# A forget-gate scan, residual rows stored as they are scaled, more filler products, and slot tables of thirteen experts kept in device memory

## What is computed

```python
def fox_shared_kv(h, kv_w, forget_bias):
    k, v, fl = jnp.split(h @ kv_w, [FD, 2 * FD], axis=-1)        # fl: 512 x 16
    log_f = jax.nn.log_sigmoid(fl + forget_bias)
    return k, v, jnp.cumsum(log_f, axis=1)                       # over the tokens

def grouped_moe(x, router_w, router_bias, w_gate, w_up, w_down):
    ...                                                          # gates: 512 x 16, two not 0
    h = silu(einsum('td,edf->tef', x, w_gate)) * einsum('td,edf->tef', x, w_up)
    return einsum('tef,efd->td', h * gates[..., None], w_down)   # 16 experts, D 1024, F 512

h = layer_norm(ALPHA * h + mix, ...)
h = layer_norm(ALPHA * h + grouped_moe(h, ...), ...)
```

## Time and profile before

| | us |
|---|---|
| median of three executions | 1234.36 |
| lowest, highest | 1230.32, 1236.86 |
| profiled execution, its own time | 1230.52 |
| its span, first to last instruction | 1228.8 |
| busy TensorE, VectorE, ScalarE, GpSimd | 1193.8, 893.2, 703.7, 183.9 |
| mean granted TensorE clock | 0.992 |

### The profile page before, as it was taken

The page is one execution under the profiler, slowest core; times in us unless marked ns, Lnnn a source line. Parts: engine busy times, 40 slices in busy tenths (PEclk is TensorE's granted clock), DMA queues, the critical chain, the costliest instruction groups (busy, mean ns, idle before and its releaser), DMA issues.

```text
span 1228.8 us, 14990 instructions
## 1 busy us (share of the span) xinstructions
PE 1193.8 (97%) x5802; PEld 945.0 (77%) x5803; DVE 893.2 (73%) x1159; ACT 703.7 (57%) x866; POOL 183.9 (15%) x158
## 2 busy tenths in 40 slices
PE   7999999999999999999999999999999999999995
PEld 5787588877888888876887766768878888888873
DVE  5275555678999998989433555675679999998886
ACT  4432523357687786774333554573267778777672
POOL 1000100211132221210000000000212222122111
PEclk9999999999999999999899999999999999999998
DMA  8223021179999999987111420322289999999973
GB/s 286 71 85 122 1 103 70 52 257 411 358 368 378 368 370 377 358 340 281 69 70 52 154 86 18 103 84 88 78 314 381 373 362 376 379 367 371 370 276 137
DMA packets 66346, 281.52 MB, mean 229 GB/s; under 512 B 12854, under 2 KB 13110, under 8 KB 41698
## 3 DMA queue, kind: packets, MB, share of 16 engines
q1 hardware_dynamic: 49248, 247.55, 53.2%
q0 software_dynamic: 12288, 28.42, 8.1%
q10 hardware_dynamic: 4738, 4.57, 1.1%
HBM read 270.99 MB, written 25.20 MB: 241 GB/s over the span
## 4 chain that ended last, share of the span: by engine, by line
PE 83%; DMA 7%; DVE 6%; issue 2%; ACT 1%; POOL 0%; DVEq 0%; SPq 0%; ACTq 0%; POOLq 0%
PE ps L717 22%; PE ps L719 22%; PE ps L718 22%; DMA ring<-in_moe_w_up_dram 4%; PE ps L885 2%; PE ps L1168 2%; PE ps L1178 2%; DVE ring_r L1613 2%; PE ps L1191 2%; DMA ring<-in_moe_w_down_dram 1%; PE ps L894 1%; DMA ring<-in_kv_w_dram 1%; PE ps L822 1%; PE ps L1099 1%; PE ps L1087 1%
## 5 line engine op out<-in xcount | busy, mean ns | idle before, releaser
L1613 DVE TENSOR_TENSOR ring_r<-ring,ring_r 128x2048 fp32r<-128x2048 f32 x128 | 291.7, 2284 | 7.8 <-ACT ring_r L1346 7.8
L1346 ACT CAST ring_r<-ring 128x2048 fp32r<-128x2048 f32 x128 | 242.6, 1927 | 15.7 <-DMA ring<-in_moe_w_gate_dram 9.8
L718 PE MATMUL ps<-ring_r,xgT_r 128*128 128x512 f32 x528 | 205.9, 390 | 0.0
L1346 ACT CAST high_r<-ring 128x2048 fp32r<-128x2048 f32 x64 | 122.2, 1913 | 113.4 <-DMA ring<-in_moe_w_up_dram 113.4
L1613 DVE TENSOR_TENSOR ring_r<-ring,high_r 128x2048 fp32r<-128x2048 f32 x64 | 146.1, 2289 | 36.3 <-ACT high_r L1346 35.9
L613 POOL DMA_INDIRECT sum_rows<-arena,tokv x28 | 57.7, 2062 | 389.6 <-ACT arena L1399 389.6
L718 PEld LDWEIGHTS ps<-ring_r,xgT_r 128*128 128x128 f32 x528 | 99.3, 188 | 18.8
L717 PE MATMUL ps<-ring_r,xgT_r 128*128 128x512 f32 x272 | 109.1, 401 | 0.2 <-DVE ring_r L1613 0.2
L719 PE MATMUL ps<-ring_r,xgT_r 128*128 128x512 f32 x272 | 106.1, 390 | 0.0
L717 PE MATMUL ps<-high_r,xgT_r 128*128 128x512 f32 x256 | 102.9, 402 | 1.2 <-DVE xgT_r L1827 1.1
L717 PE MATMUL ps<-featT,ring_r 128*128 128x512 f32 x256 | 103.8, 405 | 0.0
(11 more groups left out here) (288 smaller groups left out, 2118.8 us busy)
## 6 DMA issues: line engine op xcount, KB each, us to landing
ring<-in_moe_w_gate_dram SPq DMA_DIRECT2D x64, 1024.0 KB, 12.2
ring<-in_moe_w_up_dram SPq DMA_DIRECT2D x64, 1024.0 KB, 13.0
ring<-in_moe_w_down_dram SPq DMA_DIRECT2D x64, 1024.0 KB, 12.4
ring<-in_gla_w_in_dram SPq DMA_DIRECT2D x6, 2048.0 KB, 9.8
ring<-in_kv_w_dram SPq DMA_DIRECT2D x4, 2048.0 KB, 12.8
ring<-in_fox_w_qg_dram SPq DMA_DIRECT2D x4, 2048.0 KB, 8.1
ring<-in_gla_w_out_dram SPq DMA_DIRECT2D x2, 2048.0 KB, 7.8
h_rows<-arena POOLq DMA_DIRECT2D x8, 512.0 KB, 2.9
```

The source lines that it names most:

```text
L718: pe.matmul(o, left[0], right[1], start=False, stop=False)
L1346: act.copy(high, w).then_inc(half_high, 1)
L1613: dve.tensor_tensor(low, w, high.bitcast(F32), ALU.subtract).then_inc(half_low, 1)
```

## The change

Five things, all at once:

1. Forget gates: `narrow` gives way to 24 products (8 blocks of three) with the 16 gate columns as weights and 512 tokens moving, so the result is 16 x 512 with the heads on partitions. Bias, Abs, Exp and Ln work on 16 x 512, and one scan of VectorE over the tokens gives the cumulative sum; the ten products and ScalarE's copy are gone.
2. Three of the four residual tiles are stored to `sum_rows` by ScalarE right after each is scaled.
3. The slot tables of experts 3 to 15 are made in device memory. VectorE works out for each token the two places expert + 16 x rank (`find_picks`, ten instructions), GpSimd writes (row number, gate) there by eight indirect stores and, when they have landed, loads the whole table, 128 x 16 x 2 (`store_picks`). The tables in device memory are filled with "no row" early in the program. One-hot comparisons, table products and `take_table` of the loop are gone; `TABLES` is 3.
4. `find_picks` stands before the first expert's rows are taken, and `take_rows(0)` before `low_half(L, 2)`.
5. More filler products at the entry: three, not two, after each of three row tables, two after each of three gate tables, then three, not five.

Some semaphores are merged (`gates_left` into `gates_summed`, `ids_done` into `tbl_done`), and two constants more are set by GpSimd at the start.

```diff
+    slot_tables = [nc.dram_tensor(f"slot_table{L}", [(P + 1) * E, 2], U32).ap() for L in range(DEPTH)]
...
+            def store_picks(L):
+                pool.wait_ge(picks_known, L + 1)
+                pool.wait_ge(tables_stored, 16 * (DEPTH + 2 * T * L))
+                for t in range(T):
+                    for j in range(2):
+                        pool.sem_inc(moves, 1)
+                        pool.indirect_dma_start(out=slot_tables[L],
+                                                out_offset=bass.IndirectOffsetOnAxis(ap=pick_at[:, t, j:j + 1], axis=0),
+                                                in_=pick_row[:, t, j, :], in_offset=None, bounds_check=last_slot,
+                                                oob_is_err=False).then_inc(tables_stored, 16)
+                pool.wait_ge(tables_stored, 16 * (DEPTH + 2 * T * (L + 1)))
+                pool.dma_start(slot_tab[:, :, :], slot_tables[L][E:, :].rearrange("(p e) c -> p e c", e=E)
+                               ).then_inc(slots_loaded, 16)
+                pool.wait_ge(slots_loaded, 16 * (L + 1))
...
+                store_picks(L)
                 for e in range(E + 1):
...
                     if e + 3 < E:
-                        pool.wait_ge(tbl_ev, 2 * (E * L + e + 4))
                         pool.wait_ge(xt_done, 2 * (E * L + e + 2))
-                        gather(xg[:, (e + 3) % 2, :], tokv[:, (e + 3) % TABLES, 0:1], gathered[(e + 3) % 2])
+                        gather(xg[:, (e + 3) % 2, :], rows_of(e + 3), gathered[(e + 3) % 2])
...
-                    entry_table(e, slice(0, 2), ps[:, IDS_BANKS[e], 0:2]).then_inc(ids_done, 1)
-                    idle_products(2, 4)
+                    entry_table(e, slice(0, 2), ps[:, IDS_BANKS[e], 0:2]).then_inc(tbl_done, 1)
+                    idle_products(3, 4)
                 pe.wait_ge(rt_ready, L + 1)
                 for e in range(3):
                     entry_table(e, slice(2, 4), ps[:, 6, 2 * e:2 * e + 2]).then_inc(tbl_done, 1)
-                idle_products(5, 4)
+                    idle_products(2, 4)
+                idle_products(3, 4)
...
-                    if e + 3 < E:
-                        pe.wait_ge(hot, E * L + e + 4)
-                        pe.wait_ge(tbl_ev, 2 * (E * L + e + 3))
-                        table(e + 3, onehot[:, (e + 3) % 2, :]).then_inc(tbl_done, 1)
...
-            for t in range(T):
-                mm = narrow(t, gkf)
+            for k in range(K):
+                mm = products(ps[0:H_B, 6, :], (gkf[:, k, 0, :], gkf[:, k, 1, :]), hT_block(k, slice(0, S)), k)
             mm.then_inc(fl_done, 1)
...
                 act.mul(dealt(H[:, t, :], K), blocks(Hp[:, t, :], K), ALPHA).then_inc(h_scaled, 1)
+                if t < T - 1:
+                    begin_sums(L, t)
+
+            def begin_sums(L, t):
+                act.wait_ge(h_scaled, T * L + t + 1)
+                act.dma_start(sum_rows[t * P:(t + 1) * P, :], H[:, t, :]).then_inc(sums_begun, 16)
...
+            def find_picks(L):
+                slot_of, far, by_pick = rt[0], rt[2], at(14656 + 64 * 4, 2 * T, E)
...
+                do(dve.scalar_tensor_tensor(out=slot_of, in0=ranks[:, :, 0:E], scalar=float(E),
+                                            in1=iota_e[:, :].unsqueeze(1).to_broadcast([P, T, E]),
+                                            op0=ALU.mult, op1=ALU.add))
...
+                dve.tensor_reduce(pick_gate[:, :, :, 1], four, AX.X, ALU.add).then_inc(picks_known, 1)
...
+                find_picks(L)
+                take_rows(0)
                 low_half(L, 2)
-                take_rows(0)
...
-                    if e + 3 < E:
-                        dve.wait_ge(tbl_done, E * L + e + 2)
-                        one_hots4(dve, onehot_of(e + 3), hot, ranks, slot1, e + 3)
...
-                    dve.tensor_tensor(f_log, f_log, f_tmp, ALU.subtract).then_inc(f_ready, 1)
+                    dve.tensor_tensor_scan(cumT[0:H_B, :], f_log, f_tmp, 0.0, ALU.add, ALU.subtract).then_inc(cum_ev, 1)
```

More of the change, by code:

```diff
@@ L674, in experts @@
                     inverse_deviation(2 * L + 1, t)
+            pool.wait_ge(kt_done, 1)
+            for L in range(DEPTH):
+                pool.dma_start(slot_tables[L][E:, :].rearrange("(p e) c -> p e c", e=E), no_slots[:, :, :]
+                               ).then_inc(tables_stored, 16)
             pool.wait_ge(sq_done, T * H_A)
@@ L759, in marker @@
                           ).then_inc(w_free, frees)
-            def narrow(t, w):
-                n = 2 * w.shape[3]
-                for k in range(K):
-                    for m, part in enumerate(hT_block(k, slice(t * P, (t + 1) * P))):
-                        mm = pe.matmul(ps[:, 6, t * n:(t + 1) * n], part,
-                                       w[:, k, :, :].rearrange("p a n -> p (a n)"),
-                                       start=k == 0 and m == 0, stop=k == K - 1 and m == 1)
-                return mm
             def tail(L):
@@ L1149, in _ @@
                 unit(u, frees=1 if u == U_PAIRS - 1 else 0)
-                if u == U_FOX + T + 1:
-                    pe.wait_ge(f_ready, 1)
-                    for t in range(T):
-                        for s in range(t + 1):
-                            mm = pe.matmul(ps[0:H_B, VALUE, t * P:(t + 1) * P], f_log[:, s * H_B:(s + 1) * H_B],
-                                           upto[:, :] if s == t else one[:, :].to_broadcast([P, P]),
-                                           start=s == 0, stop=s == t)
-                    mm.then_inc(cum_done, 1)
             def scores(s):
@@ L1362, in experts @@
                 high_half(L, 5)
-                for t in range(T):
-                    act.wait_ge(h_scaled, T * L + t + 1)
-                    act.dma_start(sum_rows[t * P:(t + 1) * P, :], H[:, t, :]).then_inc(sums_begun, 16)
+                begin_sums(L, T - 1)
                 def take_hidden(e):
@@ L1873, in experts @@
                         low_half(L, half_of("down", e, 1))
[L1874 to L1885 removed]
+                    if e == E - 2:
+                        own.mark(dve.tensor_scalar(tile_base, row_id[:, :], row_id[:, 0:1], -1.0, ALU.subtract, ALU.mult))
+                        own.mark(dve.tensor_scalar(tokf, slot_tab[:, SCATTERED:, 0], 1.0, None, ALU.add))
+                        own.settle(dve)
+                        for a in range(2):
                             own.mark(dve.tensor_scalar(tokc[:, a, :], tile_base, tokf[:, a:a + 1], None, ALU.add))
```

99 lines of the change are left out of this document (53 added, 46 removed).

## The result

| | before | changed |
|---|---|---|
| median of 20 executions, us | 1230.96 | 1226.97 |
| lowest, highest | 1229.03, 1237.53 | 1219.73, 1230.42 |
| profiled execution, own time | 1230.52 | 1222.26 |
| its span | 1228.8 | 1220.6 |

The ratio is 0.995, 95% interval 0.9933 to 0.9967. It follows the means, which are 6.2 us apart; the medians are 4.0 apart. The median that was forecast, 1225.6, is 1.4 us off, and the profiled execution gained 8.3 us where 8.8 were forecast. The 20 times explain how the profiled execution can gain twice what the medians do: 9 lie from 1219.7 to 1225.0, median 1221.79, and 11 from 1226.4 to 1230.4. More than half of the executions lose some 7 us somewhere, and the profiled one isn't among them.

The account below looks back on a forecast made before the run. TensorE bounds outside the experts, DMA engines bound the whole expert stage. Gates -7.0 and experts 2 x -0.9 give -8.8 us: 1221.7 for the profiled execution, 1225.6 beside the median of three, 1234.36; range 1217 to 1242.

Parts of the forecast that it names:

- The forget gates: Layer 1's forget gates: 24 wide products replace 64 narrow ones, half clock and token-sum products go; 7.0 us saved.
- Rival C: Forget gates: the 7.0 us are taken back as attention starts on uncast weights; 1232.6 us, chance 0.10.
- The transfers decide a layer's end: Experts of both layers: the later of TensorE and DMA ends decides, and it is the DMA's: -0.9 us a layer.
- the sum had 0.9: Experts, DMA side: -3.8 for residual stores plus 2.9 for table stores, giving -0.9 us a layer.
- TensorE's 4.4 us a layer: Experts, TensorE side: -4.4 for tables, -1.2 for the stall near the end, +1.2 at the entry.
- rival A: Experts: the DMA engines can go faster, at 417 GB/s, so TensorE decides; 1218.6 us, chance 0.20.
- Residual and table stores, -3.8 and +2.9: Experts' DMA time per layer: early residual stores free 3.8 us, 1024 tiny table packets cost 2.9 us.
- Does the table come in time?: Experts' start: fourth gather, behind stores and table load, lands between 292.9 and 323.3, middle 308.1, needed at 308.4: just in time.
- the 3.5 us that I had as free of charge: Experts: lateness TensorE's side can give before it becomes the later end, 4.4 - 0.9 = 3.5 us.
- rival B: Fourth expert's rows: table late, gather 14.9 us late in each layer; 1248.4 us, chance 0.20.
- faster by more: Whole kernel: faster by over 0.5%, 6.2 us; chance 0.64.
- a layer which loses anything breaks the argument on the transfers: Sign for the experts: a layer that gains 4 us or loses any breaks the DMA argument.
- Entry and fillers: Experts' entry: more fillers and the picks start the first gate product 1.2 us later; fillers may hold layer 1's clock.

Follow-up runs that it names:

- experiment 4: The forget-gate part of the change alone, put into the kernel before: 1223.76 us, ratio 0.9926.
- exp. 9: The kernel before with the forget gates and the early residual stores only, tables by products as before: 1225.02 us, ratio 0.9931.
- exp. 2: The changed kernel with the fourth expert's table made by one-hot comparison and products, so its gather needs no table in memory: 1220.97 us, ratio 0.9904.
- exp. 5: The changed kernel with one VectorE instruction of the second expert, which reads PSUM, moved one weight subtraction later: 1219.29 us, ratio 0.9894.
- exp. 6: The kernel of exp. 2 with the ten instructions of the picks behind the first expert's rows, not ahead of them: 1222.27 us, ratio 0.9915.
- exp. 7: The kernel of exp. 2 with the entry's filler products as in the kernel before: 1220.73 us, ratio 0.9918.
- exp. 11: The kernel of exp. 5 with two filler products moved between the halves of the third tile's router products: 1219.45 us, ratio 0.9899.
- exp. 12: The kernel of exp. 5 timed once more without further edit, on another chip: 1221.23 us, ratio 0.9905.
- exp. 1: The changed kernel timed again without edit, beside the kernel before: 1229.81 us, ratio 0.9966.
- exp. 3: The changed kernel with GpSimd loading the slot table twice, one load behind the landing of the other: 1228.92 us, ratio 0.997.
- exp. 8: The kernel of exp. 2 with the four residual stores together behind the first expert's casts, as in the kernel before: 1229.83 us, ratio 0.9983.

## Why the prediction was right, and where it was not

*The forget gates.* Right in mechanism and nearly in size: 7.0 forecast, 7.4 in the trace, 8.8 in the medians of experiment 4. Rival C (the gain taken back by uncast weights) is excluded by the 9.3 us that are still there at layer 1's experts.

*The transfers decide a layer's end.* Borne out to within about 1 us. From the up issue near 287 to the first key-value weight of layer 1, and from layer 1's third up issue to the end of the span, in the profiled executions:

```
                                  layer 0   layer 1
no tables in memory:  before      264.66    302.03
                      exp. 4      263.76    301.22
                      exp. 9      264.42    300.97
tables, gather        changed     262.83    (missed)
in time:              exp. 2      264.70    298.93
                      exp. 5      262.34    300.38
                      exp. 6      263.79    299.42
                      exp. 7      264.33    300.54
                      exp. 11     262.83    299.80
                      exp. 12     264.31    300.64
tables, gather        changed     (in time) 303.42
missed:               exp. 1      269.38    302.54
                      exp. 3      266.21    302.91
residual late:        exp. 8      268.70    305.80
```

The means of the first two groups are 264.28 and 263.59 in layer 0, 0.7 us apart, and 301.41 and 299.95 in layer 1, 1.5 apart, where the sum had 0.9; single executions scatter by 1 to 2. TensorE's 4.4 us a layer were mostly given back, and rival A falls: from 465 on the up issues come 18.5 us and more apart at 371 GB/s. In the kernel before, though, the two bounds lie so close that freed transfers alone gained nothing (experiment 9).

*Residual and table stores, -3.8 and +2.9.* Their sum was about right, but they don't add up as terms. The early stores do leave the full queue: from issue to landing the median is 2.6 us, where the earlier trace rows had 15.1.

```profile
sum_rows<-resid ACTq DMA_DIRECT2D x8, 512.0 KB, 2.6
```

Early stores alone gave nothing (experiment 9), tables with late stores lost some 6 to 7 us (experiments 8 and 4), both together, with the gather in time, gained 2.5 to 4.5 (experiments 5, 12 and 4). What one frees is worth something only where the other makes TensorE fast enough to need it. The cost of the tables' packets has no clean measurement. The windows from 268 to 420 give an estimate, experiment 2 and then experiment 4:

```profile
268.00:420.00 152.00, 150.08 (x717) 124.37 (x716) 137.97 (x106) 113.97 (x98) 46.64 (x25) 1.00 1.00 367
```

```profile
268.00:420.00 152.00, 150.10 (x730) 125.19 (x729) 140.07 (x122) 114.38 (x100) 35.52 (x16) 1.00 1.00 375
```

At the same share of 1.00, 8 GB/s less over 152 us is 1.2 MB, 3.2 us; the changed kernel has 369, 2.4 us; counted in 268 to 330 alone (350 and 376 GB/s) it is 4.3. The two kernels also differ in when the residual is stored, so this is no more than an estimate. It leaves 2.9 standing as a choice between 0 and 8.3.

*Does the table come in time?* This is the step that failed. The middle of its range was good, 308.1 forecast, 305.5 measured, needed at 307.23, but by two errors against each other: the last store went out at 283.99 (282.3 in the middle), since 0.3 us lie between two issues, and the three landings took 7.1, 5.9 and 8.6 us and not 8.6 each. And I took lateness as a smooth quantity. In fact the gather that asked 1.8 us later (1.3 of them shared by VectorE) went out 8.3 us later, at 306.21 and not 297.96, because GpSimd was held behind VectorE's subtractions. The 2.24 us beside 0.99 in the earlier trace rows was a sign of that, and I read it only as a range of durations; a stronger one stood in the same trace, a gather of 4.87 us:

```profile
363.32 4.87 POOL L607 DMA_INDIRECT arena<-h_rows,tokv  x1 [0.31 <-PE ps L885]
```

Of the 3.5 us that I had as free of charge, 2 to 3 exist. At the miss the up issues fall 7.8 us (experiment 1) and 5.6 (experiment 3) behind the pace in layer 0, and 5.8 and 2.6 of these are left at its end (269.38 and 266.21 against 263.59). In layer 1 it is 4.9 to 5.8 at the miss and 2.6 to 3.5 at the end. They aren't free in full because a waiting TensorE frees no slots, so the transfers stop too (share 0.37 in 316 to 320). So rival B holds in a smaller size and in more executions than I gave it: not 14.9 us a layer with a chance of 0.2, but 3 to 6 (by the layers' ends), and, as the times and a trace of either group suggest, in layer 0 of more than half of the executions.

That the median came out near the forecast is luck, by two errors. With every gather in time the change gains 11 us and not 8.8 (medians of experiments 2, 5 and 12), and the misses take some 5 to 7 back, so that 4.0 are left by the medians, 6.2 by the means. The median of three that I started from, 1234.36, lay 3.4 above that of twenty, which hid the difference. As a ratio the forecast is 0.9929, just outside the interval. By the medians the outcome is "within", to which the prediction gave 0.23, and by the ratio it stands on the edge of "faster by more", 0.64. The prediction's own sign, that a layer which loses anything breaks the argument on the transfers, came up too (layer 0 of experiments 1 and 3, layer 1 at every missed gather); what it shows is the wait for the table, not another bound.

*The landing times.* The prediction says that even the shortest landing of the trace is 5.0 us. That holds for gathers; GpSimd's plain stores of `h_rows`, 512 KB each, landed 2.9 us after issue in the kernel before.

*Entry and fillers.* +1.2 us was too much, 0.4. The fillers show no effect on the end (experiment 7); the picks at the entry are not settled (experiment 6).

## What to carry to other kernels

When a change adds a DMA issued by GpSimd on the path, look at what VectorE does at that moment, not only at landing times: two durations for the same issue were here the sign that something held it, and moving one VectorE instruction by 2.2 us was worth some 7 us by the ratios, more than the 2.5 to 4.5 that tables and early stores together bring without a miss. Two groups of times where one was before call for a trace from each. And savings that share a bound are priced together, not one by one.

## What the runs showed of the hardware

An indirect DMA of GpSimd takes 1.0 us to issue beside an idle VectorE or one that reads PSUM (0.99 at 280.11 of the changed kernel). Beside subtractions of two SBUF tensors it waits first. Its end is then 1.0 us behind the start of a later VectorE instruction, mostly the very next one, whatever that reads: in the fourteen traces 331 gathers began beside a weight subtraction, and 286 of them got in at the next instruction although it had two SBUF inputs as well, and ended 0.94 to 1.03 us behind its start. The changed kernel's fifth gather is one; the second of the two subtractions starts near 307.1:

```profile
305.77 2.35 POOL L617 DMA_INDIRECT arena<-h_rows,slot_tab  x1 [0.30 <-issue]
```

```profile
304.92 4.49 DVE L1623 TENSOR_TENSOR ring_r<-ring,ring_r 128x2048 fp32r<-128x2048 f32 x2 [0.34 <-ACT ring_r L1361]
```

Fourteen gathers passed by one or two such instructions, and every one of these ended 1.0 us behind the start of an instruction that reads PSUM. The first three rows are long fourth gathers; in the last two the next instruction was the reader anyway.

```
             gather starts, ends      VectorE's PSUM reader starts
exp. 1       298.76, 306.21           305.20
changed      928.28, 935.07           934.03
exp. 1       940.52, 947.43           946.42
exp. 3       304.53, 306.36           305.33
exp. 5       299.35, 300.97           299.97
```

What lets one gather in between two subtractions and makes another pass them by, the runs don't tell. The Trainium skill, SBUF — State Buffer, section "Who interferes with whom", says that a VectorE instruction with two SBUF inputs contends with a GpSimd instruction that reads SBUF. The trace agrees, if reading the row numbers counts as such. The same section infers that the making of descriptors isn't held by such a `tensor_tensor`. For plain DMAs the trace agrees: GpSimd's load of the table at 291.06 took 0.60 us beside a subtraction that lasted until 292.9, about what its stores of `h_rows` take (0.58). The indirect ones are held, by up to 6.5 us.

The clock fell to half at the router's narrow products in the profiled executions of experiments 1, 3, 5, 9 and 12 and in none of the others. The changed kernel shows both, with the same program: not in its first profile, but in experiment 1, where it took 1.3 us in layer 0 and 4.5 in layer 1. In layer 0 of experiment 9 the mean granted clock is 0.57 over 250 to 262, and the first two up issues are 23.6 us apart, where the kernel before has 19.0. What tips it stays open; spreading two fillers showed no effect in the median.
